# HGRN square sums copied out of two PSUM banks, their logarithms moved behind the probabilities of unit 2, one transposed unit copied by VectorE, the first attention scores in other banks

## The chip, the cores and the metric

The kernel runs on one core of one Trainium2 chip. The metric is the device time of one execution in microseconds (us), lower is better; the time before is 1590.74 us, the median of three runs (1589.51 to 1591.55). TensorE (PE) multiplies matrices into the eight PSUM banks, ScalarE (ACT) and VectorE (DVE) read PSUM and SBUF, GpSimd (POOL) works on SBUF, and SyncE (SP) issues most DMAs.

## The reference

The reference is a two-layer encoder on 512 tokens of width 1024. A layer mixes three head groups (an HGRN2 recurrence, grouped-query attention, an S5 state-space layer), projects them back, and then runs a mixture of 32 experts. What the change touches is the end of the HGRN group and the attention:

```python
def rms_norm(x, g):
    y = xf * lax.rsqrt(jnp.mean(xf * xf, axis=-1, keepdims=True) + NORM_EPS)
    return (y * g.astype(jnp.float32)).astype(x.dtype)

# HGRN2, 4 heads of 64
o = (o_f + o_b).transpose(0, 2, 1, 3)
gate = jax.nn.silu(g.astype(jnp.float32)).reshape(B, S, HG_HEADS, HEAD_DIM)
o = rms_norm(o, norm_g) * gate

# attention, 8 query heads, 2 kv heads, blocks of 128 queries
def attend(q_blk):
    s = jnp.einsum('bkgqd,bksd->bkgqs', q_blk, kh) * scale
    p = jax.nn.softmax(s, axis=-1)
    return jnp.einsum('bkgqs,bksd->bkgqd', p, vh)
```

## The kernel before, in words

Every engine has its own program, written out by hand for each of the two layers (`tensor_program`, `scalar_program`, `vector_program`, `pool_program`, `sync_program`); semaphores tie them together. The order of instructions on an engine is the order in which the code calls its helpers, so an engine that waits holds up all that stands behind it. Everything is float32.

The input projection is computed in 26 groups of 512 columns (L636 and neighbours), group `n` in the bank that `group_bank` gives: the last two, 24 and 25, in banks 0 and 1, evicted by ACT (L1181). Between the groups stand the pieces of the HGRN recurrence and of the rotary embedding.

Then come 16 attention units, `NU = 16`: a unit is one pair of query heads and one block of 128 queries. For a unit `u`:

- PE `scores(u)` (L698): four matmuls of 512 columns in two banks, `S_BANK[u % 2]`, that is banks 0 and 1 or banks 2 and 3.
- DVE `row_max(u)` (L1650) reads both banks.
- ACT `probs(u)` (L1328): two `Exp` with the maxima as bias; the sums of the rows come out beside them. It sends `ex`, for which `scores(u + 2)` waits.
- PE `turned(u)` (L711): eight transposes of the probabilities into banks 4 and 5 (`T_BANK`).
- ACT copies both banks to SBUF (L1340), and sends `pt_e`.
- DVE inverts the sums (L1672, sends `pn`); PE `values(u)` (L720, L726) multiplies inverse sums and values into bank 6 or 7; DVE `unit_out(u)` (L1662, L1664) multiplies them, and sends `o_b`.

In its loop PE does `scores(u + 2)`, `values(u - 1)`, `turned(u)`; ACT does the copy of unit `u` and `probs(u + 2)`; DVE does the inverse of unit `u`, `row_max(u + 2)` and `unit_out(u - 1)`.

The HGRN output of the second pair of heads (`hgrn_out(1)`, L673 and L678) stands between `scores(1)` and the loop. ACT squares it and copies it (L1278, L1279). PE sums the squares of both pairs with a matmul each (`head_sums`, L684) into banks 4 and 5, `M_BANK`, the same banks as `T_BANK`. ACT then takes `Ln` of both banks and `Exp(-0.5 x)` of the results (`head_rstd`, L1284 and L1288), each with a load of its function table ahead. `turned(0)` waits for the logarithms, since they free its banks. DVE's `head_norm(p)` (L1655, L1656) multiplies the output of a pair by its inverse root and by the gate: two SCALAR_TENSOR_TENSOR of 128 x 512, all tensor inputs in SBUF, the second waiting for the first. It stands in units 1 and 2 of DVE's loop, after `row_max(u + 2)`. It sends `o_a`, for which SP waits before it loads the output projection's weights.

POOL computes the S5 matrices meanwhile. Its `times` (L2201, L2202) are TENSOR_TENSORs of 128 x 2048 and 128 x 2304, twelve in a row, from SBUF to SBUF. They start as soon as the small preparations (L2189 to L2192) are done, which wait for a DMA of S5 parameters that SP issues after the projection groups; nothing in the attention loop holds them back. They send `bc`.

After the attention PE goes on with the output projection's first parts (`early`, L790), and the S5 part.

## Time and profile before

| | |
|---|---|
| median of three runs | 1590.74 us (1589.51 to 1591.55) |
| profiled execution, its own time | 1591.55 us |
| span of the profiled execution | 1589.7 us |
| TensorE busy | 1536.3 us, 97% of the span |
| VectorE, ScalarE, GpSimd busy | 622.3, 428.5, 375.7 us |
| granted TensorE clock, mean | 0.998 |

A span is the time from the first to the last record of the core; the execution's own time is a little longer. Times in rows are from the span's start. Matmuls are pipelined, so records of PE overlap: the start of the next group says when the one before it made room. An idle time in brackets stands ahead of a row with what ended it. Layer 0's attention lies at 164 to 231 us, layer 1's at 950 to 1017 us, with the same pattern 786.0 us later.

### The profile page before, as it was taken

The numbers are of one execution on the slowest core, as the hardware profiler recorded it, in microseconds if no ns is written. First come the engines' busy times: TensorE is split into PE (matmuls) and PEld (weight loads), VectorE is DVE, ScalarE is ACT, GpSimd is POOL, SyncE is SP. The second block draws the span as 40 slices with busy tenths as digits, with TensorE's granted clock in tenths as the row PEclk, the third lists the DMA queues.
The fourth block names the chain that finished last, engine by engine and source line by source line (L and its number), as shares of the span: only waits on it lengthen the run. The fifth ranks groups of instructions, "written<-read, shape, count | busy, mean of one in ns | idle before, by whom it ended". The sixth has DMA issues, their size and how long they took to land.

```text
span 1589.7 us, 20330 instructions
## 1 busy us (share of the span) xinstructions
PE 1536.3 (97%) x8214; PEld 794.2 (50%) x8214; DVE 622.3 (39%) x1236; ACT 428.5 (27%) x766; POOL 375.7 (24%) x440
## 2 busy tenths in 40 slices
PE   8999999999999999998999999999999999999986
PEld 5655566555444444443357546655554444444432
DVE  1687546462122212311327966474522122113114
ACT  3564651211111111111235547503111111111102
POOL 5571880000000000000264638600000000000003
PEclk9999999999999999999999999999999999999999
DMA  9300403699999999999860003056999999999997
GB/s 393 144 1 14 144 4 82 267 380 420 428 426 427 428 426 427 428 426 428 329 269 1 1 27 133 1 168 267 386 425 427 425 427 427 427 427 427 428 425 287
DMA packets 57105, 470.01 MB, mean 296 GB/s; under 512 B 19321, under 2 KB 19449, under 8 KB 29330
## 3 DMA queue, kind: packets, MB, share of 16 engines
q1 hardware_dynamic: 49762, 452.37, 68.7%
q0 software_dynamic: 7104, 16.24, 2.8%
q8 instruction: 68, 1.11, 0.3%
q14 instruction: 27, 0.22, 0.0%
q10 hardware_dynamic: 144, 0.07, 0.0%
HBM read 447.69 MB, written 26.74 MB: 298 GB/s over the span
## 4 chain that ended last, share of the span: by engine, by line
PE 84%; DMA 10%; DVE 2%; ACT 2%; issue 1%; POOL 1%; DVEq 0%; SPq 0%; POOLq 0%
PE bank L1008 24%; PE bank L636 13%; PE bank L1045 11%; PE bank L998 9%; DMA ring<-wu 7%; PE bank L790 6%; PE bank L630 2%; PE bank L698 2%; PE bank L711 2%; PE bank L726 1%; PE bank L985 1%; PE bank L1032 1%; DMA expert_rows<-raw_qd,store_rows 1%; PE bank L607 1%; PE bank L624 1%
## 5 line engine op out<-in xcount | busy, mean ns | idle before, releaser
L2223 POOL DMA_INDIRECT expert_rows<-raw_qd,store_rows x60 | 58.8, 980 | 1005.6 <-ACT raw_qd L1429 850.0
L1008 PE MATMUL bank<-ring,hbuf 128*64 128x512 f32 x640 | 281.2, 593 | 8.4 <-DMA ring<-wu 8.4
L1009 PE MATMUL bank<-ring,hbuf 128*64 128x512 f32 x640 | 281.5, 593 | 0.0
L1975 DVE COPY raw_qd<-bank 128x256 f32<-128x256 f32 x64 | 27.2, 424 | 642.6 <-PE bank L1032 642.6
L636 PE MATMUL bank<-hbuf,ring 128*128 128x512 f32 x480 | 210.0, 594 | 0.0
L1008 PEld LDWEIGHTS bank<-ring,hbuf 128*64 128x64 f32 x640 | 86.7, 137 | 186.7 <-issue 186.7
L1008 PE MATMUL bank<-raw_qd,hbuf 128*64 128x512 f32 x372 | 163.7, 592 | 3.3 <-DMA hbuf<-wu 3.3
L1045 PE MATMUL bank<-ring,raw_qd 128*64 128x512 f32 x352 | 160.4, 598 | 6.4 <-DMA ring<-wd 3.3
L1047 PE MATMUL bank<-ring,raw_qd 128*64 128x512 f32 x352 | 160.5, 598 | 0.0
L998 PE MATMUL bank<-raw_qd,x 128*128 128x192 f32 x896 | 159.5, 332 | 0.0
L1422 ACT ACTIVATE raw_qd<-bank 64x512 f32<-64x512 f32 x64 | 37.8, 590 | 418.1 <-PE bank L1009 418.1
L998 PEld LDWEIGHTS bank<-raw_qd,x 128*128 128x128 f32 x896 | 144.2, 190 | 3.5
L636 PEld LDWEIGHTS bank<-hbuf,ring 128*128 128x128 f32 x480 | 90.2, 190 | 109.3 <-issue 107.6
L1009 PE MATMUL bank<-hbuf 128*64 128x512 f32 x300 | 132.9, 593 | 0.0
L1008 PEld LDWEIGHTS bank<-raw_qd,hbuf 128*64 128x64 f32 x372 | 50.6, 137 | 107.9 <-issue 107.9
L790 PE MATMUL bank<-ring,raw_qd 128*128 128x512 f32 x232 | 103.8, 595 | 0.0
L1415 ACT ACTIVATE hbuf<-bank,norm_gain 128x192 f32<-128x192 f32 x128 | 46.3, 416 | 166.6 <-PE bank L998 142.0
L1429 ACT ACTIVATE raw_qd<-bank 128x512 f32<-128x512 f32 x64 | 38.2, 597 | 195.8 <-PE bank L1047 195.8
L1045 PEld LDWEIGHTS bank<-ring,raw_qd 128*64 128x64 f32 x352 | 44.6, 136 | 91.3 <-issue 85.5
L1009 PEld LDWEIGHTS bank<-ring,hbuf 128*64 128x64 f32 x640 | 86.7, 137 | 0.0
L1045 PE MATMUL bank<-ninth_slot,raw_qd 128*64 128x512 f32 x160 | 72.9, 598 | 1.0 <-DVE raw_qd L1975 1.0
L1047 PE MATMUL bank<-ninth_slot,raw_qd 128*64 128x512 f32 x160 | 72.9, 598 | 0.0
(404 smaller groups left out, 2244.8 us busy)
## 6 DMA issues: line engine op xcount, KB each, us to landing
ring<-wd SPq DMA_DIRECT2D x42, 2048.0 KB, 20.6
ring<-wg SPq DMA_DIRECT2D x38, 2048.0 KB, 19.9
ring<-wu SPq DMA_DIRECT2D x36, 2048.0 KB, 22.6
ninth_slot<-wd SPq DMA_DIRECT2D x20, 2048.0 KB, 21.4
hbuf<-wu SPq DMA_DIRECT2D x18, 2048.0 KB, 23.7
raw_qd<-wg SPq DMA_DIRECT2D x18, 2048.0 KB, 19.1
ring<-w_in SPq DMA_DIRECT2D x8, 2048.0 KB, 18.6
raw_qd<-wg SPq DMA_DIRECT2D x6, 1792.0 KB, 12.7
```

The costliest lines, as they stand in the source:

```text
L630: last = mm(bank[:, 256 * half:256 * half + 256], hT[:, k, P * b:P * b + P], w[:, k, 256:512], start=(k == 0), stop=(k == KT - 1))
L636: last = mm(bank[:, :], w[:, k, c:c + P], hT[:, k, :], start=(k == 0), stop=(k == KT - 1))
L790: last = mm(bank[:, :], mixed[k][:, P * b:P * b + P], w_o[half][:, k, :], start=(k == tiles[0]), stop=(k == tiles[-1]))
L998: last = mm(pb[n % 2][:, GC * i:GC * i + GC], x[:, b, P * k:P * k + P], pick[:, b, :], start=(b == 0), stop=(b == NB - 1))
L1008: mm(pb[2 + par][0:CAP, :], tokens[:, k, :], gates[k], start=(k == 0), stop=(k == KT - 1))
L1009: last = mm(pb[2 + par][CAP:P, :], tokens[:, k, :], ups[k], start=(k == 0), stop=(k == KT - 1))
L1045: mm(pb[5 + par][0:CAP, :], hidT[par][:, k, :], downs[:, k, 0:512], start=(k == 0), stop=(k == FT - 1))
L1047: last = mm(pb[5 + par][CAP:P, :], hidT[par][:, k, :], downs[:, k, 512:1024], start=(k == 0), stop=(k == FT - 1))
L1415: ins = A(xT[group % 2][:, k, :], pb[bank][:, GC * i:GC * i + GC], ACT.Copy, scale=gain2[:, k:k + 1])
L1422: A(e_e, pb[2 + e % 2][0:CAP, :], ACT.Tanh, scale=0.5).then_inc(s["ee"], 1)
L1429: A(y_sb[par], pb[5 + par][:, :], ACT.Copy, scale=0.5).then_inc(s["ye"], 1)
L2223: G.indirect_dma_start(out=half_rows, out_offset=bass.IndirectOffsetOnAxis(ap=store_i[:, e:e + 1], axis=0), in_=y_sb[e % 2], in_offset=Non ...
```

## The change

- `S_BANK` is swapped: units 0, 2, 4... use banks 2 and 3, units 1, 3... banks 0 and 1. So `scores(0)` no longer waits for ACT's evictions of the groups 24 and 25; `scores(1)` does. The output projection's first part moves from bank 0 to bank 2.
- `head_sums(0)` is issued before `hgrn_out(1)`, and `scores(2)` between `hgrn_out(1)` and `head_sums(1)`.
- ACT copies the square sums out of banks 4 and 5 (`head_sum(p)`, new semaphore `ho_c`), and `turned(0)` waits for these copies, each half for its own bank.
- The logarithms (`head_logs`) read the copies in SBUF, and stand behind `probs(2)`; the roots (`head_roots`) stand in unit 2 between the copy of the transposed probabilities and `probs(4)`.
- DVE's `head_norm` moves from units 1 and 2 to units 3 and 4.
- The transposed probabilities of unit 1 are copied by DVE, after `unit_out(0)`.
- `ho_s` now counts the square and the copy of a pair one by one; `head_sums` waits for the square alone, and `values(1)`, whose bank is the HGRN output's, for the copy. The semaphore `yt` is merged into `y5`, without a move.

```diff
-        S_BANK, T_BANK, A_BANK = (0, 2), 4, (pb[6], pb[7])
+        S_BANK, T_BANK, A_BANK = (2, 0), 4, (pb[6], pb[7])
+        BY_VECTOR = 1
...
             def head_sums(p):
-                pe.wait_ge(s["ho_s"], on("ho_s") + p + 1)
+                pe.wait_ge(s["ho_s"], on("ho_s") + 2 * p + 1)
+                pe.wait_ge(s["kv_e"], on("kv_e") + HG)
...
             def scores(u):
                 if u == 0:
+                    pe.wait_ge(s["r_ln"], on("r_ln") + 5)
+                    pe.wait_ge(s["r_done"], on("r_done") + 5)
+                elif u == 1:
                     wait_evacuated(pe, layer, NG - 2)
                     wait_evacuated(pe, layer, NG - 1)
-                    pe.wait_ge(s["r_ln"], on("r_ln") + 5)
-                    pe.wait_ge(s["r_done"], on("r_done") + 5)
...
             def turned(u):
                 pe.wait_ge(s["ex"], on("ex") + u + 1)
                 if u == 0:
-                    pe.wait_ge(s["ho_s"], on("ho_s") + 2)
-                    pe.wait_ge(s["ho_r"], on("ho_r") + 1)
                     pe.wait_ge(s["hs_m"], on("hs_m") + HG)
...
                 for i in range(2):
+                    if u == 0:
+                        pe.wait_ge(s["ho_c"], on("ho_c") + i + 1)
...
             scores(0)
             scores(1)
+            head_sums(0)
             hgrn_out(1)
-            head_sums(0)
+            scores(2)
             head_sums(1)
...
             for u in range(NU):
-                if u + 2 < NU:
+                if 0 < u < NU - 2:
                     scores(u + 2)
...
-            def head_rstd():
+            def head_sum(p):
+                act.wait_ge(s["ho_m"], on("ho_m") + p + 1)
+                A(o_rs[p], M_BANK[p][:, :], ACT.Copy).then_inc(s["ho_c"], 1)
+
+            def head_logs():
+                act.wait_ge(s["ho_c"], on("ho_c") + 2)
                 for p in range(2):
-                    act.wait_ge(s["ho_m"], on("ho_m") + p + 1)
-                    ins = A(o_rs[p], M_BANK[p][:, :], ACT.Ln, bias=eps, scale=1.0 / HD)
+                    ins = A(o_rs[p], o_rs[p], ACT.Ln, bias=eps, scale=1.0 / HD)
                 ins.then_inc(s["ho_r"], 1)
+
+            def head_roots():
...
             probs(0)
             probs(1)
+            head_sum(0)
             pair_out(1)
-            head_rstd()
+            head_sum(1)
             for u in range(NU):
-                act.wait_ge(s["pt"], on("pt") + u + 1)
-                if u >= 2:
-                    act.wait_ge(s["pv"], on("pv") + u - 1)
-                A(pT_sb[u % 2], banks[:, T_BANK:T_BANK + 2, :], ACT.Copy).then_inc(s["pt_e"], 1)
+                if u != BY_VECTOR:
+                    act.wait_ge(s["pt"], on("pt") + u + 1)
+                    if u >= 2:
+                        act.wait_ge(s["pv"], on("pv") + u - 1)
+                    A(pT_sb[u % 2], banks[:, T_BANK:T_BANK + 2, :], ACT.Copy).then_inc(s["pt_e"], 1)
+                if u == 2:
+                    head_roots()
                 if u + 2 < NU:
                     probs(u + 2)
+                if u == 0:
+                    head_logs()
...
-                if u in (1, 2):
-                    head_norm(u - 1)
+                if u in (3, 4):
+                    head_norm(u - 3)
                 if u >= 1:
                     unit_out(u - 1)
+                if u == BY_VECTOR:
+                    dve.wait_ge(s["pt"], on("pt") + u + 1)
+                    V.tensor_copy(pT_sb[u % 2], banks[:, T_BANK:T_BANK + 2, :]).then_inc(s["pt_e"], 1)
```

On ScalarE, between `probs(1)` and `probs(3)` of layer 0, the order before is this (L1278 and L1279 square and copy the HGRN output, L1284 are the logarithms, L1288 the roots, L1340 the copies of transposed probabilities, L1328 the probabilities):

```order
L1278 ACTIVATE ring<-bank 128x512 [waits s_ho]
L1279 ACTIVATE ring<-bank 128x512
L1284 ACT_TABLE_LOAD
L1284 ACTIVATE ring<-bank,consts_and_pack_sb 128x512 [waits s_ho_m] x2
L1288 ACT_TABLE_LOAD
L1288 ACTIVATE ring<-ring 128x512 [waits s_ho_r]
L1288 ACTIVATE ring<-ring 128x512
L1340 ACTIVATE ring<-bank 128x1024 [waits s_pt]
L1328 ACTIVATE ring,small<-bank,small 128x512 [waits s_pt,s_mx]
```

Now it is this (L1289 are the new copies, L1284 and L1285 the square and the copy, L1294 the logarithms, L1354 the copies of transposed probabilities, L1340 now the probabilities):

```order
L1289 ACTIVATE ring<-bank 128x512 [waits s_ho_m]
L1284 ACTIVATE ring<-bank 128x512 [waits s_ho]
L1285 ACTIVATE ring<-bank 128x512
L1289 ACTIVATE ring<-bank 128x512 [waits s_ho_m]
L1354 ACTIVATE ring<-bank 128x1024 [waits s_pt]
L1340 ACTIVATE ring,small<-bank,small 128x512 [waits s_pt,s_mx]
L1340 ACTIVATE ring,small<-bank,small 128x512
L1294 ACT_TABLE_LOAD
L1294 ACTIVATE ring<-ring,consts_and_pack_sb 128x512 [waits s_ho_c]
L1294 ACTIVATE ring<-ring,consts_and_pack_sb 128x512
L1340 ACT_TABLE_LOAD [waits s_pt]
L1340 ACTIVATE ring,small<-bank,small 128x512 [waits s_mx]
```

Both table loads and the logarithms have moved from ahead of the first copy of transposed probabilities to behind the probabilities of unit 2; the roots stand further down, ahead of the probabilities of unit 4.

On VectorE, from unit 2 of the attention on, the order before is this (L1650 is the row maximum of unit 4, L1655 and L1656 are `head_norm(1)`, L1662 and L1664 `unit_out(1)`, L1672 the inverse sums):

```order
L1672 RECIPROCAL small<-small 128x2 [waits s_pv,s_ex]
L1650 TENSOR_REDUCE small<-bank 128x2 [waits s_ex,s_qk]
L1655 SCALAR_TENSOR_TENSOR ring<-ring,consts_and_pack_sb 128x512 [waits s_ho_r]
L1656 SCALAR_TENSOR_TENSOR raw_qd<-ring,raw_qd 128x512 [waits s_dve]
L1662 COPY ring<-bank 128x128 [waits s_pv]
L1664 TENSOR_TENSOR raw_qd<-bank,ring 128x128 [waits s_pn_e]
```

Now the two multiplications stand first in unit 3, and again in unit 4 (the rows begin with the inverse sums and the row maximum of unit 3; L1668 is the row maximum, L1673 and L1674 are `head_norm`):

```order
L1690 RECIPROCAL small<-small 128x2 [waits s_pv,s_ex]
L1668 TENSOR_REDUCE small<-bank 128x2 [waits s_ex,s_qk]
L1673 SCALAR_TENSOR_TENSOR ring<-ring,consts_and_pack_sb 128x512 [waits s_ho_r]
L1674 SCALAR_TENSOR_TENSOR raw_qd<-ring,raw_qd 128x512 [waits s_dve]
L1680 COPY ring<-bank 128x128 [waits s_pv]
L1682 TENSOR_TENSOR raw_qd<-bank,ring 128x128 [waits s_pn_e]
L1690 RECIPROCAL small<-small 128x2 [waits s_pv,s_ex]
L1668 TENSOR_REDUCE small<-bank 128x2 [waits s_ex,s_qk]
L1673 SCALAR_TENSOR_TENSOR ring<-ring,consts_and_pack_sb 128x512 [waits s_ho_r]
L1674 SCALAR_TENSOR_TENSOR raw_qd<-ring,raw_qd 128x512 [waits s_dve]
```

Behind them in each unit wait that unit's `unit_out`, and the inverse sums and the row maximum of the next one.

## Rows read from the trace of the kernel before

**Rows 1.** The page: busy us, share of the span and instructions of each engine.

```profile
PE 1536.3 (97%) x8214; PEld 794.2 (50%) x8214; DVE 622.3 (39%) x1236; ACT 428.5 (27%) x766; POOL 375.7 (24%) x440
```

**Rows 2.** Windows over both attentions: length, then busy us by engine, clock, DMA.

```profile
163.60:231.30 67.70, 65.09 (x608) 42.73 (x608) 35.23 (x66) 44.43 (x89) 60.16 (x25) 1.00 0.24 87
949.60:1017.40 67.80, 65.18 (x610) 42.76 (x609) 35.38 (x66) 44.43 (x89) 59.74 (x25) 1.00 0.24 87
```

**Rows 3.** Timeline of PE, layer 0: start, us, what [idle before <-releaser].

```profile
164.32 1.99 PE L698 MATMUL bank<-raw_qd 64*128 64x512 f32 x8 [0.73 <-ACT raw_qd L1181]
...
170.64 2.39 PE L684 MATMUL bank<-ring,consts_and_pack_sb 128*128 128x512 f32 x4
...
174.69 1.06 PE L711 MATMUL bank<-consts_and_pack_sb,ring 128*128 128x128 f32 x8 [0.59 <-ACT ring L1284]
...
183.23 1.13 PE L698 MATMUL bank<-raw_qd 64*128 64x512 f32 x4
...
186.55 1.13 PE L698 MATMUL bank<-raw_qd 64*128 64x512 f32 x4
...
190.49 1.13 PE L698 MATMUL bank<-raw_qd 64*128 64x512 f32 x4 [0.24 <-ACT ring L1328]
...
197.14 1.13 PE L698 MATMUL bank<-raw_qd 64*128 64x512 f32 x4
```

**Rows 4.** Timeline of ACT, layer 0, from the HGRN logarithms on.

```profile
171.87 1.28 ACT L1284 ACT_TABLE_LOAD   x1
...
173.16 1.26 ACT L1284 ACTIVATE ring<-bank,consts_and_pack_sb 128x512 f32<-128x512 f32 x2
...
174.45 1.28 ACT L1288 ACT_TABLE_LOAD   x1
...
176.80 1.00 ACT L1340 ACTIVATE ring<-bank 128x1024 f32<-128x1024 f32 x1
...
177.70 0.68 ACT L1328 ACTIVATE ring<-bank,small 128x512 f32<-128x512 f32 x1
```

**Rows 5.** Timeline of DVE and POOL, layer 0, around `head_norm(1)`.

```profile
178.87 1.55 POOL L2190 TENSOR_SCALAR ring<-ninth_slot,consts_and_pack_sb 128x288 f32<-128x288 f32 x1
...
181.08 1.23 DVE L1650 TENSOR_REDUCE small<-bank 128x2 f32<-128x1024 f32 x1 [0.94 <-PE bank L698]
...
182.22 0.74 DVE L1655 SCALAR_TENSOR_TENSOR ring<-ring,consts_and_pack_sb 128x512 f32<-128x512 f32 x1
182.30 8.67 POOL L2201 TENSOR_TENSOR ring<-ring 128x2048 f32<-128x2048 f32 x2
183.00 4.24 DVE L1656 SCALAR_TENSOR_TENSOR raw_qd<-ring,raw_qd 128x512 f32<-128x512 f32 x1
...
187.16 0.28 DVE L1662 COPY ring<-bank 128x128 f32<-128x128 f32 x1
...
191.04 3.82 POOL L2202 TENSOR_TENSOR ring<-ring 128x2048 f32<-128x2048 f32 x1
```

**Rows 6.** The chain that ended last, layer 0: start, us, what.

```profile
183.00 4.24 DVE raw_qd L1656
```

**Rows 7.** Timeline of DVE and POOL, layer 1, the same place.

```profile
968.61 4.06 POOL L2201 TENSOR_TENSOR ring<-ring 128x2048 f32<-128x2048 f32 x1
968.97 4.25 DVE L1656 SCALAR_TENSOR_TENSOR raw_qd<-ring,raw_qd 128x512 f32<-128x512 f32 x1
```

**Rows 8.** Timelines of DVE and POOL, layer 0, where both run two-input instructions in SBUF.

```profile
106.18 0.83 DVE L1568 TENSOR_TENSOR raw_qd<-raw_qd,ring 128x512 f32<-128x512 f32 x1
106.54 0.78 POOL L2152 TENSOR_TENSOR ninth_slot<-ninth_slot 128x128 f32<-128x128 f32 x1
107.04 0.83 DVE L1572 TENSOR_TENSOR raw_qd<-raw_qd,ring 128x512 f32<-128x512 f32 x1
107.40 0.78 POOL L2153 TENSOR_TENSOR ninth_slot<-ninth_slot 128x128 f32<-128x128 f32 x1
```

**Rows 9.** Windows at the span's end, columns as in Rows 2 (PE, PEld, DVE, ACT, POOL, clock, DMA).

```profile
1578.00:1581.00 3.00, 1.26 (x3) 0.19 (x2) 2.52 (x3) 2.73 (x5) 1.09 (x4) 1.00 0.45 161
1581.00:1584.00 3.00, 0.00 (x0) 0.00 (x0) 2.53 (x3) 0.70 (x2) 2.62 (x3) 0.84 0.13 53
1584.00:1587.00 3.00, 0.00 (x0) 0.00 (x0) 2.34 (x2) 0.00 (x0) 0.38 (x1) 0.50 1.01 404
```

More of the change, by code:

```diff
@@ L272, in trunk @@
             kv_e="ACT: chunk k v evacuated, after the decay rows", state="DVE: chunk states",
-            ho="PE: HGRN outputs of a pair of heads", ho_s="ACT: HGRN output of a pair, its squares",
+            ho="PE: HGRN outputs of a pair of heads", ho_s="ACT: squares of the HGRN output of a pair, the output",
             ho_m="PE: HGRN square sums", ho_r="ACT: HGRN logarithms of both pairs, then rstd of each", o_a="DVE: o_a of a pair",
@@ L276, in trunk @@
             ex="ACT: probabilities", pn="DVE: inverse sums of a unit", pt="PE: probabilities transposed",
-            pt_e="ACT: transposed probabilities evacuated", pv="PE: attention output of a unit, inverse sums by row",
+            pt_e="ACT, once DVE: transposed probabilities evacuated", ho_c="ACT: HGRN square sums evacuated", pv="PE: attention output of a unit, inverse sums by row",
             pn_e="DVE: inverse sums by row evacuated", o_b="DVE: o_b of a unit", u5="u stored, loaded by chunk, then S5 chunk matrix loaded",
@@ L285, in trunk @@
             z="DVE: S5 quarters scanned",
-            zs="PE: S5 states swapped", xs="DVE: S5 states", y5="PE: S5 outputs", y5_e="ACT: S5 outputs, first half",
-            y5_v="DVE: S5 outputs, second half", yt="PE: S5 outputs feature-major", ge="DVE: gelu argument", gx="ACT: gelu, then GLU tanh", z5="DVE: gelu",
+            zs="PE: S5 states swapped", xs="DVE: S5 states", y5="PE: S5 outputs, those feature-major", y5_e="ACT: S5 outputs, first half",
+            y5_v="DVE: S5 outputs, second half", ge="DVE: gelu argument", gx="ACT: gelu, then GLU tanh", z5="DVE: gelu",
             glu="PE: GLU products", o_c="DVE: o_c of a tile",
@@ L437, in trunk @@
         O_BANK, M_BANK = pb[7], (pb[4], pb[5])
-        S_BANK, T_BANK, A_BANK = (0, 2), 4, (pb[6], pb[7])
-        EARLY_BANK = [pb[0], pb[6]] + [pb[6 + n % 2] for n in range(2, 2 * NB)]
+        S_BANK, T_BANK, A_BANK = (2, 0), 4, (pb[6], pb[7])
+        EARLY_BANK = [pb[2], pb[6]] + [pb[6 + n % 2] for n in range(2, 2 * NB)]
         n_sb = [ring[:, 1, 3584 + P * i:3712 + P * i] for i in range(2)]
@@ L658, in hgrn_kv @@
                 if hh == 2:
-                    pe.wait_ge(s["ho_s"], on("ho_s") + 1)
+                    pe.wait_ge(s["ho_s"], on("ho_s") + 2)
                 for b in range(NB):
@@ L717, in values @@
                     pe.wait_ge(s["o_b"], on("o_b") + u - 1)
+                elif u == 1:
+                    pe.wait_ge(s["ho_s"], on("ho_s") + 4)
                 bank = A_BANK[u % 2]
@@ L768, in first_early @@
                 for k in tiles:
-                    last = mm(pb[0][:, :], mixed[k][:, 0:P], w_o[0][:, k, :], start=(k == 0), stop=(k == 5))
+                    last = mm(EARLY_BANK[0][:, :], mixed[k][:, 0:P], w_o[0][:, k, :], start=(k == 0), stop=(k == 5))
                 if tiles[-1] == 5:
@@ L896, in tensor_program @@
                 last = tr(pb[t // 4][:, P * (t % 4):P * (t % 4) + P], Y5[:, t, :, :].rearrange("p g c -> p (g c)"), ident)
-            last.then_inc(s["yt"], 1)
+            last.then_inc(s["y5"], 1)
             early(5)
@@ L1746, in vector_program @@
                           pb[5][:, :].rearrange("p (g t c) -> p g t c", g=4, t=SC)).then_inc(s["y5_v"], 1)
-            dve.wait_ge(s["yt"], on("yt") + 1)
+            dve.wait_ge(s["y5"], on("y5") + 2)
             for m in range(2):
```

6 lines of the change are left out of this document (3 added, 3 removed).

## The prediction

> **What bounds the kernel now.** I read the page first: TensorE is busy for 97% of the span and VectorE for 39% [rows 1]. So the time is the length of TensorE's own program plus its few waits, and a change can only gain what TensorE waits at the place it touches. The windows over the two attentions say how much that is: TensorE is busy for 65.1 of 67.7 us in layer 0, and for 65.2 of 67.8 in layer 1, at the full clock [rows 2]. That is 2.6 us of idle records in each, 5.2 in all, and not all of it is for this change to take. The timeline of PE shows where the waits lie: 0.73 us before the first scores, for ACT's eviction of group 25; 0.59 us before the first transposes, for the HGRN logarithms; and a period of 3.94 us (186.55 to 190.49) where the undisturbed period of a unit is 3.32 us (183.23 to 186.55, and 190.49 to 197.14 is two of 3.32) [rows 3]. ACT's timeline shows two table loads and the logarithms between the HGRN output and the first copy of transposed probabilities [rows 4]. The timeline of DVE and POOL explains the long period: DVE's second multiplication of `head_norm(1)` took 4.24 us, where the first took 0.74, while POOL was in its L2201 [rows 5]; that 4.24 us stands in the chain that ended last [rows 6], and layer 1 has it again with 4.25 [rows 7].
>
> **How DVE and POOL hinder each other.** A pair of DVE and POOL instructions that both read two operands from SBUF never ran together here. L1656 (start 183.00) ended when the first of POOL's two L2201 ended, plus its own 0.7 us; the two L2201 then took 8.67 us instead of two times 3.9 (3.82 is the undisturbed L2202) [rows 5]. With short instructions one sees who comes next: two dependent DVE instructions, 0.83 us each, start 0.86 us apart, and one POOL instruction of 0.78 us, short of its own work, is interleaved between each two [rows 8]. So after each such DVE instruction POOL's next one gets in first, and a dependent DVE instruction waits for the whole of it. DVE instructions that read PSUM are not held: L1650 and L1662 keep their 1.23 and 0.28 us [rows 5]. In the kernel before, three of the four multiplications of a layer were done before POOL began its row of twelve long instructions; only the fourth met one.
>
> **The change, part by part**, in layer 0's times.
>
> 1. *Front.* `scores(0)` goes back by 0.73, to 163.6. From there to the end of the HGRN output it is 6.3 us (164.32 to 170.64), plus 0.9 for the head sum now in front [rows 3]; then `scores(2)` and the second head sum, 1.06 each as between the starts of a unit's groups (a record of 1.13 overlaps the next): 173.0. `turned(0)` now waits for a PSUM copy of 128 x 512 by ACT, which I take as 0.6 (one of 128 x 1024 takes 1.00, one exponential of 128 x 512 takes 0.68 [rows 4]), and its second half ends at 174.2. Before, it ended at 175.7 [rows 3]. The gain at this point is 1.5 us.
>
> 2. *ACT behind it.* Nothing is saved in work: the table loads and logarithms are moved, two copies of 0.6 are added, one eviction of 1.0 goes to DVE. From 174.3 ACT does a copy (0.9), two exponentials (0.7 each, 1.4), table 1.28, logarithms 1.26, table 1.28, two exponentials (1.4): 7.5 us [rows 4], so `ex(3)` comes at 181.8 and `scores(5)`, which waits for it, starts at 182.0, where it started at 183.23 [rows 3]. The gain that is left is 1.2 us. The roots (1.2) come after, in unit 2, and leave `scores(6)` at 185.3, 1.2 early, and `scores(7)` at 188.7. The page "ScalarE: Activation LUTs" of the Trainium skill (What ACT_TABLE_LOAD costs) counts a drain of about 1.38 us on top of each load, 2.66 us in all. By it two switches would cost ACT 2.8 us more here and the sum below would be an estimated 5.5 us higher over both layers; in this trace the load is followed by its function 0.01 us later, so the row is used.
>
> 3. *DVE's eviction.* A reduction over the same 128 x 1024 from PSUM takes 1.23 us [rows 5], and ACT's copy 1.00 [rows 4]; I take 1.2 us, from 177.7. DVE has some 1.4 us idle in a period of 3.32, and nothing late stands behind it. Bounds: 0 and 1.2 us, taken as 0, since ACT's chain ends later.
>
> 4. *`head_norm` in units 3 and 4.* This decides. POOL's first L2201 started at 182.30 [rows 5]; the L2190 before it had been held for 0.55 us (1.55 where others take 1.00) by a multiplication that is now gone, so it starts at 181.75. From then to about 233 POOL runs long instructions with gaps of 0.1 us. DVE is done with the row maxima of unit 5 at 184.3 (scores at 182.0, 1.1 for them, 1.2 for the reduction). Then, in order: the first multiplication waits until 181.75 + 3.9 = 185.65 and ends at 186.4; the second waits for all of the next POOL instruction, 4.24 as in the row: 190.6; `unit_out(2)`, the inverse sums and the row maxima of unit 6 take 0.6 + 0.2 + 1.2: 192.6; the third multiplication finds POOL in an instruction that started at about 190.5 and waits until 194.4, done at 195.1; the fourth takes 4.24: 199.4; `unit_out(3)`, inverse, row maxima of unit 7: 201.3; ACT's exponentials for unit 7: 202.8; `scores(9)`: 203.0. Before, `scores(9)` started at 197.14 [rows 3]. Behind that both kernels run one unit in 3.32 us, because DVE and ACT have no more to do in a unit than before. So layer 0 loses 5.9 us, front gain included. Before, the lag of one 4.24 us stall had cost 0.62 us, since some 3 to 4 us of slack cover it; here 12 us fall into two units, and one slack covers them once.
>
>    In layer 1 POOL's first L2201 starts at 968.61 [rows 7], which is 182.6 in layer 0's times, some 0.3 less when it is not held before: 182.3, so the first multiplication waits 0.5 longer. Layer 1 loses 6.3 us.
>
> 5. *Downstream.* POOL is held four times instead of twice for 0.5 us, and ends near 233.5 instead of 233.0; its results are wanted by PE after the attention, which now ends near 237. The weights of the output projection are requested when `o_a` is complete, at 199 instead of 187, and are wanted at the first early projection, after 225: hidden. Everything after the attention hangs on it in TensorE's order, the weight loads of the experts too, so I let the whole delay through.
>
> **Sum.** 5.9 + 6.3 = 12.2, say 12 us. The profiled execution, 1591.55 us, becomes 1603.6; against the median of 1590.74 that is **1602.8 us**, slower by 0.76%. Bounds: the first multiplication of a layer may meet POOL at a gap (nothing) or at a start (3.9), where I took 1.3 to 1.9. That is 3 us less to 4.5 more over both layers: 1599.5 to 1607.5.
>
> **Rivals.** A measurement of this kernel can tell about 0.2%, 3.2 us, from no change.
>
> - *R1, faster: DVE's stalls stay in the slack.* If the multiplications found gaps, or if POOL's row were over by then, the front gain of 1.2 us, plus 0.6 for the stall that is gone, plus what the smoother order gives, would stay: 2 us a layer, 4 in all, 1586.7 us. For it: each wait of TensorE that the change names is real [rows 3]. Against: POOL's program is unchanged, and its long instructions cover 182 to 233 with gaps of 0.1 us [rows 5, 7].
> - *R2, only the first of two multiplications waits*, because DVE keeps what it has got for the dependent one. Then a layer's two stalls are 1.3 and up to 3.2 us, which the slack of 3 to 4 us nearly covers: 1.2 gained and about 0.5 lost in each, 1589 us. It decides from the point where DVE's next instruction is ready before POOL's. Against it: the strict alternation [rows 8].
> - *R3, slower still: the clock falls.* In item 4 TensorE stands still between `scores(8)` (over at about 195.3) and the inverse sums of unit 5 (at about 200.2). At the end of the span TensorE's records stop in the window 1578 to 1581, and the granted clock averages 0.84 in the next and 0.50 in the one after, that is it went from 2.4 to 1.2 GHz [rows 9]. If it falls in a wait of 5 us, a unit at half speed costs 3.3 us more, in both layers: 1609.4 us. "TensorE: Matmul & The Clock Gate" of the Trainium skill (Why this matters for your kernels) says the same of idle stretches, and advises against long waits between bursts of matmuls.
>
> **How the numbers follow.** Item 4 as reckoned 0.62, R3 0.15, R2 0.10, R1 0.10, and 0.03 for something else that is slower. Slower by over 0.2%: 0.62 + 0.15 + 0.03 = 0.80. R1 is faster, and so is a third of R2: 0.13. The rest of R2 is no change: 0.07. The range takes in item 4's bounds, more slack than I gave DVE (below), and R3 (above): 1595 to 1611; it leaves out R1 and R2, 0.20.
>
> **What would show it.** In the profile after: the four multiplications of each layer (L1673, L1674) with about 2, 4.2, 2.6 and 4.2 us, and a TensorE wait of 4 to 5 us for DVE ahead of the inverse sums of unit 5; `scores(5)` about 1.2 us early, `scores(9)` about 6 us late; 3.32 us a unit after that; nothing changed in the experts' part. I am wrong if the multiplications that depend on another take under 1 us (R2), if they are long but `scores(9)` is not late (more slack than I see), or if `scores(5)` is already late, which would mean that ACT and not DVE pays.

## The result, and the profile after

The changed kernel takes 1603.44 us, the median of four runs (1603.02 to 1604.07), against 1590.74 us of the kernel before: ratio 1.0078, 95% interval 1.0063 to 1.0093. By the ratio it is 12.4 us slower (10.0 to 14.8), by the two medians 12.7; the forecast was 1602.8 us and slower. A fourth execution of the kernel before, at 1634.21 us, was in a slower state that comes now and then whatever the kernel, and such executions are left out of the ratios. The profiled execution spans 1601.9 us against 1589.7.

The page of the changed kernel, engines as in [rows 1]:

```profile
PE 1540.0 (96%) x8214; PEld 796.7 (50%) x8214; DVE 637.6 (40%) x1238; ACT 429.3 (27%) x768; POOL 375.7 (23%) x440
```

TensorE's busy time grew by 3.7 us although its work is the same: a sign that some of it ran slower. VectorE's grew by 15.3 us for two more copies of 1.23 us (one per layer): the rest is waiting inside instructions, which a profile counts as busy.

Windows over both attentions, and three short ones in layer 0 (length, then busy us of PE, PEld, DVE, ACT, POOL, granted clock, DMA), to be laid beside [rows 2]:

```profile
163.60:238.00 74.40, 66.79 (x607) 44.41 (x606) 42.95 (x69) 44.12 (x89) 63.11 (x27) 0.95 0.22 79
949.60:1025.00 75.40, 67.20 (x582) 43.25 (x582) 44.78 (x67) 43.70 (x89) 66.69 (x30) 0.95 0.22 78
195.00:198.00 3.00, 0.00 (x0) 0.00 (x0) 3.00 (x1) 0.00 (x0) 3.00 (x1) 0.72 0.00 0
198.00:201.00 3.00, 1.77 (x18) 1.79 (x19) 2.93 (x9) 0.69 (x3) 2.92 (x2) 0.50 0.52 120
```

Timeline of VectorE, layer 0 (`head_norm` is L1673 and L1674, the inverse sums L1690), as in [rows 5]:

```profile
184.05 1.75 DVE L1673 SCALAR_TENSOR_TENSOR ring<-ring,consts_and_pack_sb 128x512 f32<-128x512 f32 x1
185.84 4.24 DVE L1674 SCALAR_TENSOR_TENSOR raw_qd<-ring,raw_qd 128x512 f32<-128x512 f32 x1
...
191.72 2.58 DVE L1673 SCALAR_TENSOR_TENSOR ring<-ring,consts_and_pack_sb 128x512 f32<-128x512 f32 x1
194.34 4.22 DVE L1674 SCALAR_TENSOR_TENSOR raw_qd<-ring,raw_qd 128x512 f32<-128x512 f32 x1
...
199.01 0.15 DVE L1690 RECIPROCAL small<-small 128x2 f32<-128x2 f32 x1
```

Timeline of POOL, the same stretch, one row per instruction up to 193.83:

```profile
181.38 3.87 POOL L2222 TENSOR_TENSOR ring<-ring 128x2048 f32<-128x2048 f32 x1
185.33 4.20 POOL L2222 TENSOR_TENSOR ring<-ring 128x2048 f32<-128x2048 f32 x1
189.61 4.14 POOL L2223 TENSOR_TENSOR ring<-ring 128x2048 f32<-128x2048 f32 x1
193.83 8.45 POOL L2222 TENSOR_TENSOR ring<-ring 128x2048 f32<-128x2048 f32 x2
```

Timeline of TensorE, as in [rows 3] (L701 scores, L725 inverse sums, L731 values, L714 transposes):

```profile
162.87 1.99 PE L701 MATMUL bank<-raw_qd 64*128 64x512 f32 x8
...
181.74 1.13 PE L701 MATMUL bank<-raw_qd 64*128 64x512 f32 x4 [1.10 <-ACT ring L1340]
...
190.75 0.44 PE L725 MATMUL bank<-consts_and_pack_sb,small 128*64 128x128 f32 x4 [1.24 <-DVE small L1690]
...
199.23 0.69 PE L725 MATMUL bank<-consts_and_pack_sb,small 128*64 128x128 f32 x4 [4.77 <-DVE small L1690]
199.69 1.94 PE L731 MATMUL bank<-ring,raw_qd 128*64 128x128 f32 x16
201.56 1.86 PE L714 MATMUL bank<-consts_and_pack_sb,ring 128*128 128x128 f32 x8
203.35 1.13 PE L701 MATMUL bank<-raw_qd 64*128 64x512 f32 x4
```

The forecast chain is there link by link: four multiplications of 1.75, 4.24, 2.58 and 4.22 us, where a free one takes 0.7; TensorE waits 1.24 us for the inverse sums of unit 4 and 4.77 us for those of unit 5; and the clock, which had fallen to 0.50 (1.2 GHz) by then, lets the next 16 matmuls take 1.94 us and the eight transposes 1.86, where 1.04 and 1.09 are normal.

**Where the 12.2 us of the span lie.** From the end of group 25's matmuls to the start of `scores(9)` it is 33.55 us before (163.59 to 197.14, 0.73 of it waiting) and 40.41 after (162.94 to 203.35): 6.86 us in layer 0. Layer 1, read the same way, has 33.52 and 40.95: 7.43 us. After `scores(9)` both kernels take 3.32 us a unit. These 14.3 us shrink to 12.2, since the profiled execution of the changed kernel began its attention 0.65 us earlier (162.94 against 163.59), and took 1.5 us less between the two attentions. I take both as scatter and not as the change, which touches nothing there but one bank: from unit 15 of the first attention to the second one it took between 730.7 and 732.5 us in the eight profiles of this study in which the clock did not fall there and POOL was not held back, the changed kernel 731.0 and the kernel before 732.5.

### The profile page after: what moved, and what is told of

Read it like the earlier page. It is cut to its first block, busy times and chain, and to the rows that moved or that the text cites. A ratio compares the mean times of both kernels' runs of the same rounds, so it can differ in the third digit from the quotient of the medians.

```text
span 1601.9 us, 20338 instructions
## 1 busy us (share of the span) xinstructions
PE 1540.0 (96%) x8214; PEld 796.7 (50%) x8214; DVE 637.6 (40%) x1238; ACT 429.3 (27%) x768; POOL 375.7 (23%) x440
## 4 chain that ended last, share of the span: by engine, by line
PE 84%; DMA 9%; DVE 4%; ACT 1%; issue 1%; POOL 1%; DVEq 0%; SPq 0%; POOLq 0%; ACTq 0%
PE bank L1014 24%; PE bank L637 13%; PE bank L1051 11%; PE bank L1004 9%; DMA ring<-wu 7%; PE bank L796 6%; PE bank L631 2%; PE bank L714 2%; PE bank L701 2%; PE bank L731 2%; PE bank L991 1%; PE bank L1038 1%; DVE raw_qd L1674 1%; DMA expert_rows<-raw_qd,store_rows 1%; PE bank L625 1%; PE bank L608 1%
```

## The experiments

T1 is the theory of the prediction's item 4: VectorE's multiplications in units 3 and 4 meet POOL's long instructions, and the second of each pair waits for a whole one. T2, its rival, puts the loss elsewhere in the change. "The wait" in the third column is TensorE's before `scores(0)`; the times after it are measured from the start of `scores(0)`, two rows of a TensorE timeline each (layer 0 alone where one is given). Where there is no wait, `scores(0)` starts 0.07 us before the last record of group 25 ends, as pipelined matmuls do. So a version without the wait is ahead of one with it by 0.8 us at `scores(0)`, and a sum of the columns understates that by 0.07; differences in the text are measured from the end of group 25. The two kernels "one multiplication per two units" and "gate product early" have the same attention to 0.01 us and ratios 0.0014 apart, so a difference of 0.1% between two ratios says nothing by itself here, and the traces decide.

| version | ratio to before | the wait | to `scores(5)` | to `scores(9)`, layers 0, 1 |
|---|---|---|---|---|
| before | 1 | 0.73 | 18.91 | 32.82, 32.78 |
| changed | 1.0078 [1.0063, 1.0093] | 0 | 18.87 | 40.48, 41.02 |
| before, norm in units 3 and 4 | 1.0088 [1.0064, 1.0113] | 0.73 | 19.00 | 39.50, 39.77 |
| one multiplication per two units | 0.9974 [0.9964, 0.9984] | 0 | 18.86 | 32.17, 32.17 |
| POOL waits | 1.0010 [0.9997, 1.0023] | 0 | 18.87 | 32.17, 32.17 |
| 24 idle matmuls | 1.0081 [1.0062, 1.0099] | 0 | 18.86 | 39.87, 41.66 |
| 16 idle matmuls | 1.0081 [1.0066, 1.0097] | 0 | 18.87 | 39.33, 40.19 |
| gate product early | 0.9988 [0.9979, 0.9998] | 0 | 18.87 | 32.17, 32.17 |
| the same, ScalarE copies unit 1 | 0.9997 [0.9988, 1.0007] | 0 | 19.77 | 33.07, 33.08 |
| before, with the new banks alone | 0.9988 [0.9979, 0.9997] | 0 | 18.86 | 32.93, 32.21 |
| gate product early, old banks | 0.9991 [0.9982, 1.0000] | 0.73 | 18.73 | 32.03, 32.02 |
| gate product early, two copies by VectorE | 0.9967 [0.9955, 0.9978] | 0 | 18.02 | 31.41, 31.41 |
| one per two units, two copies by VectorE | 0.9973 [0.9963, 0.9984] | 0 | 18.01 | 31.33, 31.34 |

### The kernel before with `head_norm` in units 3 and 4

```diff
-                if u in (1, 2):
-                    head_norm(u - 1)
+                if u in (3, 4):
+                    head_norm(u - 3)
```

> The kernel before with one edit: head_norm in units 3 and 4 of VectorE's loop instead of 1 and 2. Theory T1 (the loss comes from four SBUF multiplications that each wait for one of GpSimd's long instructions): nearly all of the loss is here already, three of the four multiplications take 2.5 to 4.2 us, ratio to before 1.006 to 1.008 (1601 to 1603 us). Theory T2 (the loss comes from ScalarE, whose table loads and logarithms now stand between the probabilities, or from the copy given to VectorE): this kernel has none of that, ratio 1.000 to 1.001.

Measured: 1604.09 us. VectorE, layer 0:

```profile
185.14 0.74 DVE L1655 SCALAR_TENSOR_TENSOR ring<-ring,consts_and_pack_sb 128x512 f32<-128x512 f32 x1
185.91 4.25 DVE L1656 SCALAR_TENSOR_TENSOR raw_qd<-ring,raw_qd 128x512 f32<-128x512 f32 x1
191.80 2.59 DVE L1655 SCALAR_TENSOR_TENSOR ring<-ring,consts_and_pack_sb 128x512 f32<-128x512 f32 x1
194.42 4.22 DVE L1656 SCALAR_TENSOR_TENSOR raw_qd<-ring,raw_qd 128x512 f32<-128x512 f32 x1
```

Two edited lines bring the whole loss, with the same wait of 4.77 us on TensorE and the same slow values behind it. The time is 1 us above the range that T1 gave, and of the four multiplications three are long, as it said. The rest of the change costs nothing; T2 falls.

### One multiplication per two units

The changed kernel with its four multiplications in units 3, 5, 7 and 9, so that none follows the one that it depends on.

```diff
-                if u in (3, 4):
-                    head_norm(u - 3)
+                if u in (3, 7):
+                    head_norm((u - 3) // 4)
+                if u in (5, 9):
+                    head_gate((u - 5) // 4)
```

`head_gate(p)` is the second multiplication, taken out of `head_norm(p)`; its wait for the first one goes with it.

> The changed kernel, the four multiplications one by one in units 3, 5, 7 and 9 instead of two in 3 and two in 4. They still wait for GpSimd, up to 4.2 us each. T1, with a slack of 3 to 4 us on VectorE that refills within two units: no TensorE wait for VectorE over 0.5 us, the gain of the front stays, 1586 to 1588 us, ratio 0.997 to 0.998. If the waits cost as such, wherever they stand: 1600 us or more. T2: 1603 us, as the changed kernel.

Measured: 1587.55 us, faster than both kernels. VectorE, layer 0:

```profile
185.04 1.96 DVE L1676 SCALAR_TENSOR_TENSOR ring<-ring,consts_and_pack_sb 128x512 f32<-128x512 f32 x1
...
191.69 3.47 DVE L1680 SCALAR_TENSOR_TENSOR raw_qd<-ring,raw_qd 128x512 f32<-128x512 f32 x1
...
198.52 0.93 DVE L1676 SCALAR_TENSOR_TENSOR ring<-ring,consts_and_pack_sb 128x512 f32<-128x512 f32 x1
...
204.99 2.63 DVE L1680 SCALAR_TENSOR_TENSOR raw_qd<-ring,raw_qd 128x512 f32<-128x512 f32 x1
```

The same four instructions still meet POOL and take up to 3.47 us, and TensorE waits for none of them: `scores(9)` comes 8.3 us earlier than in the changed kernel. What costs is two held instructions within one unit, more than its slack.

### POOL held back until the multiplications are done

```diff
             pool.wait_ge(s["q_silu"], on("q_silu") + 4)
+            pool.wait_ge(s["o_a"], on("o_a") + 2)
```

> The changed kernel, GpSimd's row of twelve long instructions begins only when both pairs are multiplied (it waits for o_a). T1: the four multiplications take 0.7 to 0.8 us, TensorE does not wait in the attention after unit 3, its scores of unit 9 start 9 us earlier than in the changed kernel; but GpSimd ends some 7 us later and TensorE and VectorE then wait 3 to 5 us for it behind the attention, so 1592 to 1598 us. T2: the attention is as long as in the changed kernel, and with the later GpSimd 1603 us or more.

Measured: 1593.01 us. All four multiplications take 0.74 or 0.69 us, and the attention is undisturbed. POOL's instructions are thereby shown as what holds VectorE. The price shows in three waits of the whole trace (engine, line, waited for: us in total, times, longest us):

```profile
ACT ring L1372 <- POOL hbuf L2223: 23.0, 2, 11.5
POOL ring L2222 <- DVE raw_qd L1674: 14.5, 2, 7.5
DVE ring L1717 <- POOL hbuf L2223: 7.0, 2, 3.5
```

POOL waits up to 7.5 us, and the S5 part behind the attention is late for it. TensorE, which sets the time, waits less than they do: 0.64 us for POOL (L837) and 0.67 us for ScalarE (L863) in layer 0, and the same within 0.01 us in layer 1. In layer 0 its clock also falls to 0.50 at 245.7 us, behind these two waits. The two attentions take 17.2 us less than in the changed kernel (8.3 and 8.9), and the time is 10.8 us lower by the ratios: holding POOL gives back over a third of what it saves.

### Idle matmuls in TensorE's long wait

```diff
+                if u == 6:
+                    pe.wait_ge(s["pt_e"], on("pt_e") + 6)
+                    keep_running(24, 4, slice(0, P), ident)
                 if u >= 1:
                     values(u - 1)
```

> The changed kernel with 24 idle matmuls of 128 columns (results unused, bank 4, 3.1 us) in TensorE's wait ahead of the values of unit 5. If the granted clock fell in that wait because TensorE had nothing to do, it now stays at 1.00 and the values and transposes behind it take 1.04 and 1.09 us instead of 1.94 and 1.86: 1.8 us less in each layer, 1599.9 us, ratio to the changed kernel 0.998. If the clock falls for another reason: 1603.4 us.

> The changed kernel with 16 idle matmuls of 128 columns in the 4.8 us wait of TensorE; 24 of them took 5.63 us, that is 0.117 us for each of 48 records, and ended 0.7 us after the wait was over. By that row 16 take 3.75 us and end 0.3 us before the wait does. If the fall of the clock costs what its rows say (0.9 us at the probabilities' transposes and 0.8 at the products), the clock stays at 1.00, values 5 start with the release, scores 9 come 1.7 us earlier than in the changed kernel in each layer where the clock had fallen for this wait, and the time is 1600 to 1602, ratio to the kernel before 1.005 to 1.0065. If the clock in the profile costs the program nothing (something later ends at the same time anyway): 1603 to 1604.5, ratio 1.007 to 1.008.

Measured: 1604.88 us with 24 of them, and 1603.64 us with 16. The idle matmuls write a bank that nothing reads then. The 24 took 5.63 us and not 3.1, and ran past the end of the wait: 0.7 us in layer 0. TensorE with 16, layer 0 and then layer 1:

```profile
195.49 3.84 PE L588 MATMUL bank<-consts_and_pack_sb 128*128 128x128 f32 x32
200.34 0.44 PE L725 MATMUL bank<-consts_and_pack_sb,small 128*64 128x128 f32 x4 [1.01 <-DVE small L1693]
200.59 1.06 PE L731 MATMUL bank<-ring,raw_qd 128*64 128x128 f32 x16
...
985.31 0.44 PE L725 MATMUL bank<-consts_and_pack_sb,small 128*64 128x128 f32 x4 [2.48 <-DVE small L1693]
985.56 1.67 PE L731 MATMUL bank<-ring,raw_qd 128*64 128x128 f32 x16
```

Windows of the same run:

```profile
200.00:205.00 5.00, 4.42 (x50) 3.27 (x52) 4.53 (x11) 3.58 (x9) 4.92 (x2) 1.00 0.90 311
785.00:790.00 5.00, 4.90 (x16) 1.25 (x12) 2.74 (x3) 0.06 (x1) 4.08 (x4) 0.71 0.96 324
985.00:990.00 5.00, 4.69 (x32) 3.50 (x32) 4.97 (x5) 2.28 (x5) 4.92 (x2) 0.66 0.00 0
```

Where the clock held, the price of its fall can be read off: from the end of the fourth multiplication to `scores(9)` it is 3.26 us here (199.66 to 202.92) and 4.79 in the changed kernel (198.56 to 203.35). So a fall costs 1.5 us in this place. `scores(9)` comes 1.15 us earlier than in the changed kernel in layer 0 and 0.83 in layer 1. But the time did not measurably come down: the ratio is 1.0081 (1.0066 to 1.0097) against 1.0078, which neither shows nor excludes a gain of 2 us. In layer 1 the clock fell one unit earlier, behind a wait of 2.48 us that the changed kernel has as 1.83 at the full clock. It fell once more in the experts' part, at 784.5 us, in a wait of 2.37 us for a weight load (`wd`) that the changed kernel has as 0.83, and where that one shows 1.00. The profile took 2.3 us more between the attentions than the changed kernel's, where the attentions had gained 2.0. The kernel with 24 has a fall in layer 1's attention too (behind 2.25 us), one in the experts' part at another place (759.2 us, behind a wait of 1.98 us for weights), and a third behind the second attention. So these kernels have as many falls as the changed one or more, in other places, and the expectation of 1600 to 1602 us missed. Why the weights came later in these profiles, the runs don't tell (five other profiles of this study have falls outside the attention too, see the end).

### The gate product made early

```diff
+            def head_gated(p):
+
+                dve.wait_ge(s["ho_s"], on("ho_s") + 2 * p + 2)
+                link(STT(out=o_sb[p], in0=o_sb[p], scalar=pcol("hgrn_g"), in1=hg[p], op0=ALU.mult, op1=ALU.mult))
+
             def head_norm(p):
-                link(STT(out=o_sb[p], in0=o_sb[p], scalar=pcol("hgrn_g"), in1=o_rs[p], op0=ALU.mult, op1=ALU.mult))
-                STT(out=hq[p], in0=o_sb[p], scalar=0.5, in1=hg[p], op0=ALU.mult, op1=ALU.mult).then_inc(s["o_a"], 1)
+                STT(out=hq[p], in0=o_sb[p], scalar=0.5, in1=o_rs[p], op0=ALU.mult, op1=ALU.mult).then_inc(s["o_a"], 1)
```

`head_gated(0)` stands ahead of unit 0 and `head_gated(1)` in unit 0, both before POOL's long row; `head_norm` stays in units 3 and 4.

> The changed kernel, but the product of a head's output with its weight and its gate is made early (of pair 0 before unit 0, of pair 1 in unit 0), so that only one 128x512 multiplication per pair, the one by the root, is left in units 3 and 4. T1 (the loss is the second, linked multiplication of each pair, which waits behind POOL's 4.2 us instruction and finds the shared access taken again): the two that are left take about 2 and 2.5 us, PE waits for them less than 1 us in a layer, its clock stays at 1.00, and the time is 1586 to 1589, ratio 0.996 to 0.999. The rival T3 (what costs is that POOL's long instructions run there at all, and any 128x512 of VectorE in units 3 and 4 takes 4.2 us): each takes 4.2 us, PE waits 1.8 us per pair, and the time is 1594 to 1598.

Measured: 1588.68 us. VectorE, layer 0:

```profile
172.59 0.74 DVE L1673 SCALAR_TENSOR_TENSOR ring<-ring,consts_and_pack_sb,raw_qd 128x512 f32<-128x512 f32 x1
...
183.98 1.76 DVE L1678 SCALAR_TENSOR_TENSOR raw_qd<-ring 128x512 f32<-128x512 f32 x1
...
187.38 2.65 DVE L1678 SCALAR_TENSOR_TENSOR raw_qd<-ring 128x512 f32<-128x512 f32 x1
```

As T1 has it: a single multiplication per unit waits for the rest of POOL's instruction only, in the same two units, and TensorE has no wait for VectorE. T3 falls. The times of the attention are to 0.01 us those of the kernel with one multiplication per two units; that its ratio is 0.0014 higher does not come from there (this profile has two falls of the clock outside the attention, see the end).

### The same, with unit 1 copied by ScalarE

```diff
-        BY_VECTOR = 1
+        BY_VECTOR = -1
```

> The previous kernel (gate product early), but the transposed probabilities of unit 1 are copied by ScalarE again and not by VectorE. T1 by its own sum: VectorE's copy lets ScalarE's queue, with two table loads and two logarithms in it, get to probabilities 3 about 1.3 to 1.6 us earlier, so without it scores 5 start about 1.5 us later in each layer, and the time is 2 to 5 us above that of the previous kernel (ratio to it 1.001 to 1.003), about 1589 to 1592. The rival (the copy's place does not matter, since ScalarE catches up behind it): within 1 us of the previous kernel.

Measured: 1590.21 us, 1.5 us more, which is 0.90 us per layer in the trace (19.77 against 18.87 to `scores(5)`). That is just ScalarE's copy, which stands between the logarithms and the second table load and pushes the load back by 0.9 us; nothing further follows from it. I had set 1.5, and a time 2 to 5 us higher; neither expectation is met. VectorE's copy earns its place, by 0.9 us a layer.

### The new banks alone, and all but the banks

The first is the kernel before with this (and the bank of the output projection's first part moved along with them):

```diff
-        S_BANK, T_BANK, A_BANK = (0, 2), 4, (pb[6], pb[7])
+        S_BANK, T_BANK, A_BANK = (2, 0), 4, (pb[6], pb[7])
...
                 if u == 0:
-                    wait_evacuated(pe, layer, NG - 2)
-                    wait_evacuated(pe, layer, NG - 1)
                     pe.wait_ge(s["r_ln"], on("r_ln") + 5)
                     pe.wait_ge(s["r_done"], on("r_done") + 5)
+                elif u == 1:
+                    wait_evacuated(pe, layer, NG - 2)
+                    wait_evacuated(pe, layer, NG - 1)
```

> The kernel before with one part of the change only: the first attention scores in banks 2 and 3, so that they wait for the root of the last rows and not for the last two evictions, which scores 1 wait for. T1: scores 0 start 0.7 us earlier in each layer, but transposing probabilities 0 still waits for the logarithms of the square sums behind output 1, which waits for the same things as before, so nothing or at most 0.7 us per layer is gained: 1590.4 to 1591.9 against 1591.9 of the kernel before in the earlier runs, ratio 0.999 to 1.000. The rival (the banks are what brings the front of the stage its 1.5 us): 1588.9 or less, ratio 0.998.

The second takes exactly this back out of the version with the early gate product.

> The version with the gate product made early, but the first attention scores in their old banks 0 and 1 again, behind the last two evictions. The banks alone brought scores 5 forward by 0.85 us in the kernel before, and the whole change brings them forward by 0.8. Theory T6 (the banks are all that the front of the stage gains; the square sums' copies, the logarithms behind probabilities 2 and VectorE's copy balance the ACT work that they move): scores 5 start 0 to 0.2 us from where they start in the kernel before, the time is 1.5 us above the version with the new banks and within 1 us of the kernel before, ratio 0.9995 to 1.0005. The rival (my prediction's sum, which gave the front 1.2 us at scores 5, of which the banks are 0.73): 0.5 us per layer is left, ratio 0.9990 to 0.9995.

Measured: 1588.54 and 1589.26 us. TensorE with the banks alone, layer 0:

```profile
163.52 1.99 PE L699 MATMUL bank<-raw_qd 64*128 64x512 f32 x8
...
182.38 1.13 PE L699 MATMUL bank<-raw_qd 64*128 64x512 f32 x4
```

and with all but the banks:

```profile
164.62 1.99 PE L700 MATMUL bank<-raw_qd 64*128 64x512 f32 x8 [0.73 <-ACT raw_qd L1186]
...
183.35 1.13 PE L700 MATMUL bank<-raw_qd 64*128 64x512 f32 x4 [1.10 <-ACT ring L1339]
```

With the banks alone `scores(5)` comes 0.85 us earlier than before (183.23, [rows 3]): the wait of 0.73 us is passed through whole, because the HGRN output stands behind `scores(0)` and `scores(1)` in TensorE's order, and the logarithms behind that. My expectation had held it back. The whole change gains 0.84 us there (18.80 us from the end of group 25, against 19.64), that is no more than the banks alone. At `scores(9)` the kernel with the banks alone is 0.7 us ahead in layer 0 and 1.4 in layer 1. The difference is the stall of `head_norm(1)`: in layer 0 it is there as before (a unit of 4.10 us, where it was 3.94), and in layer 1 VectorE's second multiplication, earlier than before, is done in 0.79 us before POOL's long row begins, and the stall is gone. Without the banks it comes only 0.18 us earlier (18.73 against 18.91). So the square sums' copies, the later logarithms and VectorE's copy together bring the front of the stage next to nothing (T6): what `turned(0)` gains is given back at `scores(5)`, in the 1.10 us wait for ScalarE. The second kernel is nevertheless 0.8 us per layer ahead at `scores(9)`, since the kernel before has its own wait there, the period of 3.94 us that the early gate product ends; I had left that out of the expectation, whose ratio of 0.9995 or more missed.

### Two copies by VectorE

```diff
-        BY_VECTOR = 1
+        BY_VECTOR = (0, 1)
...
-                if u != BY_VECTOR:
+                if u not in BY_VECTOR:
...
-                if u == BY_VECTOR:
+                if u in BY_VECTOR:
```

> The version with the gate product made early, but VectorE copies the transposed probabilities of units 0 and 1, not of unit 1 alone. In that version's trace scores 5 wait 1.10 us for ScalarE's probabilities 3, which stand behind its copy of unit 0, probabilities 2, two table loads and two logarithms, and the copy of unit 1 was worth 0.91 us per layer there. Theory T4 (this queue is what the stage's front waits for): the wait of 1.10 us falls to 0.3 or less, scores 5 start 0.8 to 1.0 us earlier in each layer, and the time is 1.5 to 2 us below the version with the early gate product: ratio to the kernel before 0.997 to 0.998. The rival T5 (VectorE's queue is as full: its copy of unit 0 pushes its row maxima of units 3 and 4 back, and the wait only changes its name): within 0.5 us of that version, ratio 0.9985 to 0.9995.

> The version with the four multiplications in units 3, 5, 7 and 9, but with VectorE's copies of units 0 and 1. T4: its wait of 1.1 us at scores 5 goes, scores 5 start 0.8 to 1.0 us earlier in each layer, and the time is 1.5 to 2 us below that version, whose ratio to the kernel before was 0.9974: 0.996 to 0.997, the fastest of all. T5: as that version, 0.997 to 0.998.

Measured: 1584.67 us with the early gate product, the lowest median of all, 0.33% below the kernel before (0.22 to 0.45%); and 1586.03 us with one multiplication per two units. TensorE of the first, layer 0:

```profile
162.58 1.99 PE L701 MATMUL bank<-raw_qd 64*128 64x512 f32 x8
...
180.60 1.13 PE L701 MATMUL bank<-raw_qd 64*128 64x512 f32 x4
184.01 1.13 PE L701 MATMUL bank<-raw_qd 64*128 64x512 f32 x4
```

The wait of 1.10 us is gone in both, and `scores(5)` comes 0.85 us earlier in each layer. ScalarE's queue, with two table loads in it, was what the front waited for (T4). In the traces both gain the same, 1.5 to 1.7 us over two layers; in the ratios the first gains 0.0021 on its parent and the second 0.0001, where both should have gained 0.001. So of these two kernels the times don't say which is faster: their intervals overlap, and the second's attention is the shorter by 0.07 us.

## Why the prediction was right, step by step

**Item 1, the front.** Right in kind, a little too large: the second half of `turned(0)` ends at 173.88 in a profile that runs 0.65 us early, so at 174.5, where 174.2 was forecast. The gain there is 1.2 us and not 1.5.

**Item 2, ScalarE behind it.** The error is handed on. I gave `scores(5)` a gain of 1.2 us; it is 0.84 (18.80 against 19.64 from the end of group 25), and the new banks alone bring 0.85. All the other parts without the banks bring 0.18. The table loads cost what the row said:

```profile
176.29 1.28 ACT L1294 ACT_TABLE_LOAD   x1
177.59 1.33 ACT L1294 ACTIVATE ring<-ring,consts_and_pack_sb 128x512 f32<-128x512 f32 x2
178.94 1.28 ACT L1340 ACT_TABLE_LOAD   x1
```

The drain of 1.38 us that the page "ScalarE: Activation LUTs" of the Trainium skill (What ACT_TABLE_LOAD costs) adds to each load is not seen here either: the logarithms start 0.02 us after their load.

**Item 3, VectorE's copy.** 1.23 us at 177.24, hidden, as forecast. Its own worth, 0.90 us per layer, was in item 2's sum and not named.

**Item 4, the multiplications.** With 0.65 us added to the profile's times, the four end at 186.5, 190.7, 195.0 and 199.2; the forecast had 186.4, 190.6, 195.1 and 199.4. The alternation is shown: the second of each pair took 4.22 to 4.24 us in both layers, and the kernel with POOL held back took 0.69. The page "SBUF — State Buffer" of the Trainium skill (SBUF: two separate sides) says that of a VectorE instruction with two SBUF inputs and one of GpSimd the first to start holds the shared pair of ports for its whole length. The trace agrees, and this, not a preference for POOL, is why the prediction's "POOL's next one gets in first" came true: whoever came first went first, both ways. The first multiplication, there since 184.05, went ahead of the POOL instruction that starts at 185.33, since it had waited longer. That POOL instruction was then in line 0.5 us before the second multiplication, which cannot start before the first one's end and starts at 185.84. In the kernel with the banks alone, POOL was first by 0.02 us, and that was enough (layer 0):

```profile
182.13 3.87 POOL L2202 TENSOR_TENSOR ring<-ring 128x2048 f32<-128x2048 f32 x1
...
182.15 4.40 DVE L1657 SCALAR_TENSOR_TENSOR raw_qd<-ring,raw_qd 128x512 f32<-128x512 f32 x1
```

In every profile a multiplication that found a long POOL instruction at work ended 0.55 to 0.57 us after that one's end. Nor is the prediction quite right that in the kernel before only the fourth multiplication met one: the third (182.22) overlaps the first L2201 (182.30) and keeps its 0.74 us, because it came 0.08 us ahead [rows 5]. From the fourth multiplication's end to `scores(9)` I had put 3.6 us, and at the full clock it is 3.26. So the stall term was 5.9 us and is 5.3 (6.86 less 1.53 for the clock), and in layer 1 it was 6.3 and is 5.9, with the price of the clock taken over from layer 0. The bounds of the sum are a little off: 3.2 us less and 4.6 more than 1602.8 are 1599.6 and 1607.4.

**Item 5, downstream.** The delay went through whole; 3.32 us a unit after `scores(9)`, no new wait behind the attention.

**R3, the clock.** I held this and item 4 apart, as if one excluded the other; both came true. The clock did fall in the wait of 4.77 us, in both layers, but a fall costs 1.5 us here, not 3.3, for two reasons that the rows show: it was back at 1.00 when `scores(9)` ran, and of the 1.9 us that the slow records lose (0.25, 0.90 and 0.77) 0.4 is hidden, for at the full clock `scores(9)` has to wait 0.25 us for ScalarE's probabilities (at 202.92, with 16 idle matmuls). That the wait costs more than its own length is also what "TensorE: Matmul & The Clock Gate" of the Trainium skill (Why this matters for your kernels) warns of.

**R1 and R2** are refuted in the changed kernel. R2 was to decide where VectorE's next instruction is ready before POOL's, and a dependent one never was: POOL's came some 0.5 us before it each time. But the 1589 us of R2 is about what comes out once only single multiplications wait: 1588.68.

So the number was right partly by luck. The stages lost 14.3 us in the profile, 11.2 from the stalls and 3.1 from the clock; I had put 12.2 and 0. The profiled execution got 2.1 us back elsewhere, by what I take as scatter. The difference of 12.4 us by the ratio has an interval of 10.0 to 14.8 us, which holds both 12.2 and 14.3.

## What to carry to other kernels

Before you move a two-input VectorE instruction on SBUF, look at what POOL runs at the new place: if POOL's run back to back with inputs in SBUF too, as these did, each such instruction waits for the rest of POOL's, and one that depends on it comes too late for the gap and waits for a whole further one. Spread them, one per unit of slack, or do one factor of the product before POOL starts; then the same waits cost nothing. And split a change of several parts before judging it: here a bank swap alone was worth 0.1%, and one misplaced pair of lines hid it under a loss of 0.8%.

## What the runs showed that I had not expected

- Idle matmuls of 128 columns cost 0.117 to 0.120 us for each of their records, two records per matmul (5.63 us for 48, 3.84 for 32), nearly twice what I had set for the first of these runs.
- In the attentions the granted clock stayed at 1.00 behind waits of 1.24, 1.61 and 1.83 us, and was down behind waits of 2.25, 2.48 and 4.77 us. The length of the wait does not decide alone: with the gate product early and the old banks, the clock stayed at 1.00 behind a wait of 2.12 us at 1504 us. Seven of the thirteen profiles also show falls outside the attention, five of them at 325 to 330 us or, 785 us later, at 1110 to 1115 (1128 with 24 idle matmuls), in a place that the edits don't touch: each begins 1.0 to 1.6 us behind a wait of 1.8 us for VectorE, which all thirteen profiles have there in both layers, most of them without a fall. The kernel before has none in its profile. With a fall, and POOL not held back, the stretch between the attentions took 732.9 to 733.3 us; without, 730.7 to 732.5. That is a part of the scatter between runs, of 0.1 to 0.2%.
- In the last kernel a multiplication took 4.10 us alone in its unit and TensorE did not wait. So one unit's slack covers at least 3.4 us of holding. In the changed kernel the first pair was held for 4.6 us and TensorE waited 1.24, in layer 1 for 5.2 and 1.83: 3.3 us covered in both. That bears out the 3 to 4 us of the prediction.

Windows of the kernel with the early gate product, at that place of either layer, show such a fall:

```profile
325.00:330.00 5.00, 5.00 (x17) 3.03 (x17) 4.29 (x19) 0.00 (x0) 0.00 (x0) 0.66 1.02 436
1110.00:1115.00 5.00, 5.00 (x17) 3.08 (x17) 4.28 (x19) 0.00 (x0) 0.00 (x0) 0.66 1.01 431
```

Open: why the clock falls at 325 us in some profiles and not in others, behind the same wait.
